# Layer 1's convolution stage: two gate tiles computed as one Strassen pair, with the conditioning tiles moved to an earlier stage

## The chip, the cores and the metric

The kernel runs on one core of a Trainium2 chip. The time is the device time of one execution in microseconds (us); the time before is the median of three runs. TensorE is PE in the rows (its weight loads are PEld), VectorE is DVE, ScalarE is ACT, GpSimd is POOL and the queue that issues the weight loads is SP.

## What is computed

The reference is two transformer blocks in fp32, with model width 1024 and 256 tokens: `first_block` (four mixer branches, a merge, a feed-forward part), then `second_block`, which runs two layers over 256 context tokens and 256 latent tokens. In the second of these layers (layer 1) only the 256 latent tokens are still needed. The part at issue is the mixer's convolution branch and the gated sums beside it:

```python
def _conv_module(glu, p):
    a, g = jnp.split(glu, 2, axis=-1)
    y = a * jax.nn.sigmoid(g)
    y = lax.conv_general_dilated(y, p['conv_w_dw'], (1,), [(pad, pad)], ...)   # depthwise, 31 taps
    y = jax.nn.silu(_layernorm(y, p['conv_ln_g'], p['conv_ln_b']))
    return y @ p['w_conv_o']
...
    g_att, g_gla, g_conv = jnp.split(jax.nn.sigmoid(gates), N_BRANCH_2, axis=-1)
    return (g_att * y_att + g_gla * y_gla + g_conv * y_conv) @ p['w_out']
```

Here `glu` and `gates` are columns of one projection of the normalised input, and `y_att`, `y_gla` are projections of the attention's and the recurrence's output. Apart from that, `silu(c) @ w_ada` gives the modulation of the layer norms; it needs only the condition vectors.

## The kernel before

Activations lie feature-major: a tile is 128 features on the partitions by the tokens, eight tiles are a full width of 1024. Weights come from a stream of tiles of 128 output features by 1024 inputs (512 KB) into eight slots `W[0]` to `W[7]`; SP issues the load of a slot when the counter `unit` says that the tile before it there has been used. `project` (L609 to L617, matmuls on L613) multiplies one weight tile by eight chunks of the input: 8 matmuls, each of which is two records in the trace.

The program is a list of phases, each with a number of turns, and every engine has a function for each phase. Each engine runs its own instructions in the order in which its function writes them, with waits on counting semaphores in between: `done` waits for this turn's event, `before` for that of the turn before, `earlier` for one of an earlier phase. Most phases begin with a wait for all engines (`phase_done`); PE goes ahead of it in those that are listed under `ahead`, the convolution stage among them.

The phases that matter here:
- `merge1` (first block): 16 tiles of gated sums in Strassen products over 128 columns (`product`, L841, and the loop on L891); a turn of it makes one tile.
- `gla`: the recurrence. Its last instruction on DVE is L3588.
- `conv`, layer 1: 8 turns, one for each tile of 128 channels. On PE (L1690) six tiles of weights by 256 tokens: the two halves of the GLU, gate and projection of the attention, gate and projection of the recurrence. ACT (L2348) makes three sigmoids (L2352, L2356). DVE (L3591) makes the GLU product (L3598), the 31 taps in two alternating sums (L3609, L3611, L3613), adds them up (L3616, L3618), handles one tile of `w_ada` (`ada_tile`, `ada_keep`, L2652 to L2671), and makes the gated sums into `MX` (L3626, L3629, L3630).
- `conv_norm`, layer 1: the mean over the convolution's output (L1784), the norm, and the eight tiles of the third gate on PE. Two of these stand ahead of the mean.
- `conv`, layer 0, computes its six tiles, over 512 tokens, with Strassen pairs already (`conv_strassen` on PE and ACT, sums of weights on L3637 to L3642).

A Strassen pair takes two weight tiles a and b (rows of a 2 x 2 block matrix, whose columns are the even and odd chunks of the inputs) and the left and right half of the tokens. Seven products of four matmuls each over half the tokens take the place of eight. They need four sums of weights (`w_summed0`), four sums of the input (`t_summed`), and copies of an accumulating bank at three points, which ACT makes (`hold`).

Of the kernel before, what the change touches and what calls it, by code (L numbers as in the profile page):

```python
# [19 lines left out]
ALU = mybir.AluOpType  # L20
# [3 lines left out]
P = 128  # L24
D = 1024
KC = D // P
# [25 lines left out]
ADA_TURNS = {"out1": (2, 0, 4), "down1": (4, 0, 5), "attend": (3, 0, 4), "attend_last": (3, 0, 4), "up2": (10, 0, 2),  # L52
             "attend1": (2, 0, 4), "attend1_last": (2, 0, 4), "conv1": (8, 0, 1)}
# [155 lines left out]
def program(nc, params, consts, stream, ada, cond, x_in, mem_in, ctx_in, out, counted):  # L209
    plan = phases()  # L210
    with ExitStack() as ctx:
# [302 lines left out]
        def split(c0):  # L514
# [23 lines left out]
        H_SUMS, G_SUMS = 17, 17 + 4 + 2 * QUADS  # L538
# [4 lines left out]
                 for v in (SQF, WORK[:, 2048:6144])]  # L543
        q_parts = [[v[:, i * S:(i + 1) * S].rearrange("p (j t) -> p j t", j=2) for i in range(8)]
                   for v in (WORK[:, 0:2048], MXF[:, 2048:4096])]
        conv_even, conv_odd = ([YG[:, FT * T2 + (2 * i + p) * S:FT * T2 + (2 * i + p + 1) * S] for p in range(2)]
# [58 lines left out]
        def _(pe):  # L605
# [1084 lines left out]
            def conv(s):  # L1690

                cols = slice(first_column(s.layer), T2)
                n = T2 - cols.start
                pe.wait_ge(*s.before("glu"))
                for u in range(2):
                    project(s, u, bank[u][:, 0:n], cols)
                pe.wait_ge(*s.earlier("gla_end", 0))
                for b in range(2):
                    pe.wait_ge(*s.before(f"gate{b}"))
                    project(s, 2 + 2 * b, bank[2 + 2 * b][:, 0:n], cols)  # L1700
                    pe.wait_ge(*s.before(f"mixed{b}"))
                    project(s, 3 + 2 * b, bank[3 + 2 * b][:, 0:n], cols, src=Y2[b])
# [68 lines left out]
            def conv_norm_first(s):  # L1771
# [3 lines left out]
                def gate(c):  # L1775
                    project(s, c, bank[2 + (c + 3 + s.layer) % 6][:, 0:n], cols)

                one, two = (2, 3) if s.layer else (4, 5)
                for c in range(one):
                    if s.layer == 0:  # L1780
                        pe.wait_ge(*s.earlier(("acc_taken0", "first_taken0", "cross_taken0", "acc_taken1")[c], 0))
                    gate(c)
# [5 lines left out]
                for c in range(two, KC):  # L1788
                    if c >= 6:
# [7 lines left out]
                     "gla": (gla_begin, gla_middle, gla_end), "conv": conv, "merge2": merge2, ("merge2", 0): merge_strassen,  # L1797
# [10 lines left out]
        def _(act):  # L1808
# [393 lines left out]
            def layernorm(s, dest, scale, shift):  # L2202
# [17 lines left out]
                for c in range(KC if conv else LATE):  # L2220
# [5 lines left out]
                    if conv:  # L2226
# [3 lines left out]
                        act.activation(sg_conv[:, c, 0:n], bank[2 + (c + 3 + s.layer) % 6][:, 0:n], ACT.Sigmoid)\  # L2230
# [117 lines left out]
            def conv(s):  # L2348
# [82 lines left out]
        def _(dve):  # L2431
# [241 lines left out]
            def merge1(s):  # L2673
# [77 lines left out]
                for t in range(1, 16):  # L2751
# [12 lines left out]
                    if t == 3:  # L2764
                        condition()
# [1219 lines left out]
```

## Time and profile before

| | |
|---|---|
| median of 3 runs | 3032.07 us (3031.69 to 3032.41) |
| the profiled execution | 3033.64 us, its span 3031.8 us |
| PE busy | 2973.9 us, 98% of the span |
| DVE busy | 1909.4 us, 63% |
| ACT busy | 739.2 us, 24% |
| granted TensorE clock | 0.998 of full speed |
| PE's share of the chain that ended last | 94% |

The span is the part of the execution in which engines worked; 1.8 us of the execution's time lie around it. Busy time of PE is modelled, so a busy PE is not PE at its peak, and successive rows of PE overlap: the pace is read from the distance between starts. "x16" is a number of records merged into one row.

### The profile page before, as it was taken

How to read it: one execution, taken by the hardware profiler on the slowest of the kernel's cores; microseconds unless marked ns; L12 is line 12 of the kernel's file. 1: busy time of each engine (PE TensorE's matmuls, PEld its weight loads, DVE VectorE, ACT ScalarE, POOL GpSimd, SP SyncE). 2: the span in 40 equal slices, each digit the busy share in tenths (PEclk: the TensorE clock that was granted, in tenths of full speed). 3: DMA queues.
4: the chain of work that ended last, by engine and by line, in shares of the span. 5: the costliest groups of instructions: out<-in, count | busy, mean ns of one | idle time of the engine just before them, and what ended most of it. 6: DMA issues, size and time to landing. Idle time of an engine off the chain costs nothing.

```text
span 3031.8 us, 45316 instructions
## 1 busy us (share of the span) xinstructions
PE 2973.9 (98%) x15958; PEld 2451.2 (81%) x15958; DVE 1909.4 (63%) x3765; ACT 739.2 (24%) x1786; POOL 62.8 (2%) x109
## 2 busy tenths in 40 slices
PE   9999999999999999999999999999999999999998
PEld 8888889989985566667775888888866778887998
DVE  4456326667656777768886566665357667863665
ACT  3334212212213333311113041110043431021111
POOL 0000000000010000000000000000000000000000
PEclk9999999999999999999999999999999999999999
DMA  5243334554562311112222114332223123434443
GB/s 194 93 149 111 139 125 168 170 208 163 198 227 104 127 53 50 63 63 83 83 83 89 63 49 146 125 125 90 90 92 119 65 86 129 176 132 153 153 150 115
DMA packets 105049, 363.97 MB, mean 120 GB/s; under 512 B 11488, under 2 KB 17632, under 8 KB 104800
## 3 DMA queue, kind: packets, MB, share of 16 engines
q1 hardware_dynamic: 90832, 310.94, 29.5%
q0 software_dynamic: 14096, 51.39, 4.8%
q8 instruction: 80, 1.31, 0.2%
q14 instruction: 41, 0.34, 0.0%
HBM read 361.23 MB, written 1.05 MB: 119 GB/s over the span
## 4 chain that ended last, share of the span: by engine, by line
PE 94%; DVE 3%; issue 1%; ACT 1%; DMA 1%; DVEq 0%; ACTq 0%; SPq 0%
PE bank L613 25%; PE bank L1126 7%; PE bank L1290 6%; PE bank L1708 5%; PE bank L841 5%; PE bank L1365 4%; PE bank L1592 4%; PE bank L1483 3%; PE bank L624 3%; PE bank L1606 2%; PE bank L1302 2%; PE bank L1456 2%; PE bank L1045 1%; PE bank L1651 1%; PE bank L1168 1%
## 5 line engine op out<-in xcount | busy, mean ns | idle before, releaser
L613 PE MATMUL bank<-H,W 128*128 128x256 f32 (+1 forms) x2048 | 497.3, 400 | 2.9 <-issue 2.8
L613 PEld LDWEIGHTS bank<-H,W 128*128 128x128 f32 x2048 | 386.9, 190 | 99.8 <-issue 52.0
L613 PE MATMUL bank<-YG,W 128*128 128x256 f32 (+1 forms) x912 | 258.9, 439 | 1.3 <-issue 0.8
L613 PEld LDWEIGHTS bank<-YG,W 128*128 128x128 f32 x912 | 172.9, 190 | 74.0 <-issue 56.6
L1483 PE MATMUL bank<-H,W 128*128 128x512 f32 (+1 forms) x320 | 119.4, 509 | 2.5 <-ACT H L2224 2.5
L1592 PE MATMUL bank<-W,H 128*128 128x256 f32 x512 | 118.8, 383 | 0.0
L1592 PEld LDWEIGHTS bank<-W,H 128*128 128x128 f32 x512 | 96.0, 193 | 13.8 <-issue 1.9
L1290 PE MATMUL bank<-MX,SQ 128*128 128x256 f32 x480 | 105.2, 379 | 0.0
L1290 PEld LDWEIGHTS bank<-MX,SQ 128*128 128x128 f32 x480 | 91.2, 190 | 12.4
L1483 PEld LDWEIGHTS bank<-H,W 128*128 128x128 f32 x320 | 58.8, 190 | 45.1 <-issue 38.2
L3655 DVE SCALAR_TENSOR_TENSOR YG<-WORK,PR,YG 128x512 f32 (+1 forms) x120 | 89.7, 747 | 0.0
L624 PEld LDWEIGHTS bank<-W,H 128*128 128x128 f32 x768 | 88.7, 192 | 0.8
L624 PE MATMUL bank<-W,H 128*128 128x128 f32 x768 | 89.0, 275 | 0.0
L1606 PE MATMUL bank<-H,W 128*128 128x512 f32 (+1 forms) x256 | 87.9, 486 | 0.0
L3655 DVE SCALAR_TENSOR_TENSOR WORK<-WORK,PR 128x512 f32<-128x512 f32 x112 | 83.7, 747 | 0.0
L1811 ACT ACT_TABLE_LOAD x21 | 26.9, 1283 | 213.7 <-DVEq L309 211.6
L1126 PE MATMUL bank<-H,W 128*128 128x128 f32 x640 | 77.7, 275 | 0.0
L1126 PEld LDWEIGHTS bank<-H,W 128*128 128x128 f32 x640 | 74.7, 192 | 0.1
L324 ACT ACTIVATE WORK<-bank,rowmax 128x128 f32<-128x128 f32 (+2 forms) x88 | 46.1, 530 | 117.3 <-DVE rowmax L317 117.3
L1708 PE MATMUL bank<-H,W 128*128 128x256 f32 x320 | 71.8, 379 | 0.3 <-issue 0.3
L1302 PE MATMUL bank<-H,W 128*128 128x256 f32 x320 | 70.8, 379 | 0.5 <-issue 0.5
L317 DVE TENSOR_REDUCE rowmax<-bank 128x1 f32<-128x128 f32 (+2 forms) x88 | 41.2, 494 | 46.0 <-PE bank L785 24.8
(633 smaller groups left out, 5841.8 us busy)
## 6 DMA issues: line engine op xcount, KB each, us to landing
W<-stream SPq DMA_DIRECT2D x556, 512.0 KB, 3.3
WORK<-ada POOLq DMA_DIRECT2D x44, 512.0 KB, 4.5
YG<-ada POOLq DMA_DIRECT2D x40, 512.0 KB, 3.6
W<-stream SPq DMA_DIRECT2D x24, 384.0 KB, 3.7
SQ<-ada POOLq DMA_DIRECT2D x12, 512.0 KB, 7.2
W<-stream SPq DMA_DIRECT2D x16, 128.0 KB, 2.3
CN<-consts SPq DMA_DIRECT2D x1, 1984.0 KB, 15.5
X<-x_in SPq DMA_DIRECT2D x2, 512.0 KB, 5.4
```

The costliest lines, as they stand in the source:

```text
L613: m = pe.matmul(out_ap, W[u][:, c, :], src[:, c, cols], start=first and c == 0, stop=last and c == k - 1)
L624: m = pe.matmul(o, H[:, c, col0 + t * P:col0 + (t + 1) * P], W[u][:, c, :], start=c == 0, stop=c == KC - 1)
L841: m = pe.matmul(out, w[:, c, :], b[:, c, :], start=first and c == 0, stop=c == KC // 2 - 1, skip_group_check=True)
L1126: m = pe.matmul(out, w[:, c, :], b[:, c, :], start=first and c == 0, stop=c == KC // 2 - 1, skip_group_check=True)
L1290: m = pe.matmul(out, w[:, c, :], b[:, c, :], start=first and c == 0, stop=c == KC // 2 - 1, skip_group_check=not first)
L1302: m = pe.matmul((acc, top)[c % 2][j], W[j][:, c, :], H[:, c, left], start=c < 2, stop=c >= KC - 2)
L1365: ends[q] = pe.matmul(out, w[q][:, c, :], b[:, 4 * q + c, :], start=first and q == 0 and c == 0, stop=q == 2 and c == n - 1, skip_group_ch ...
L1483: m = pe.matmul(out_bank[:, 0:T2 - cols.start], W[i][:, c, :], H[:, c, cols], start=c == 0, stop=c == KC - 1)
L1592: m = pe.matmul(o, H[:, c, t * P:(t + 1) * P], slots[:, 3:5, c, :], start=c == 0, stop=c == KC - 1)
L1606: m = pe.matmul(bank[6 + u][:, 0:n], W[5 + u][:, c, :], H[:, c, c0:T2], start=c == 0, stop=c == KC - 1)
L1708: m = pe.matmul(out, w[:, c, :], b[:, c, :], start=first and c == 0, stop=c == KC // 2 - 1, skip_group_check=not first)
L3655: o = dve.scalar_tensor_tensor(sums[tap % 2], src, w, sums[tap % 2], ALU.mult, ALU.add)
```

## The change

- `conv`, layer 1: the two gate tiles (slots 0 and 4) become one Strassen pair over two halves of 128 tokens. The other four tiles stay as they were. The GLU tiles (slots 2 and 3) stand at the beginning of a turn's loop body; the pair and the attention's projection for the next turn are opened at its end. The stream's order of tiles is changed to match.
- ACT: three copies and four sigmoids of 128 columns and one sigmoid of 256 per turn, instead of three sigmoids of 256.
- DVE: four sums of weights per turn, three sums that take the products out of the banks, and the taps in pieces between them: 3, 3, 6, 8 and 11. The pieces of 8 and 11 stand behind the first sum of the next turn's pair.
- The eight tiles of `w_ada` that this stage handled go to `merge1`, one in each of eight turns, with their loads (issued by POOL).
- `conv_norm`, layer 1: three tiles of the third gate ahead of the mean instead of two.

Cut to its core:

```diff
-ADA_TURNS = {"out1": (2, 0, 4), "down1": (4, 0, 5), "attend": (3, 0, 4), "attend_last": (3, 0, 4), "up2": (10, 0, 2),
-             "attend1": (2, 0, 4), "attend1_last": (2, 0, 4), "conv1": (8, 0, 1)}
+MERGE_ADA = (4, 5, 7, 8, 9, 11, 12, 13)
+ADA_TURNS = {"merge1": (8, 0, 1), "out1": (2, 0, 4), "down1": (4, 0, 5), "attend": (3, 0, 4), "attend_last": (3, 0, 4), "up2": (10, 0, 2),
+             "attend1": (2, 0, 4), "attend1_last": (2, 0, 4)}
...
+            def conv_halves():
...
+                def open_pair(s, begins=False):
+                    acc, top, cross = (bank[5 + i][:, 0:P] for i in range(3))
...
+                    product(acc, a[:, EVEN, :], H[:, EVEN, left], first=True).then_inc(*s.tick("p10"))
...
+                    pe.wait_ge(*s.before("first_taken0"))
+                    product(top, a[:, ODD, :], H[:, ODD, left], first=True).then_inc(*s.tick("p20"))
+                    pe.wait_ge(tally.sem("t_summed"), CONV_SUMS + 2)
+                    pe.wait_ge(*s.done("p1_held0"))
+                    pe.wait_ge(*s.done("w_summed0", 1))
+                    product(acc, sums[1], late_t[1]).then_inc(*s.tick("v20"))
+                    pe.wait_ge(*s.before("cross_taken0"))
+                    pe.wait_ge(*s.done("w_summed0", 3))
+                    product(cross, sums[0], late_t[0], first=True).then_inc(*s.tick("unit"))
+                    pe.wait_ge(tally.sem("t_summed"), CONV_SUMS + 3)
+                    pe.wait_ge(*s.done("v2_held0"))
+                    for c in range(KC // 2):
+                        m = pe.matmul(acc, sums[2][:, c, :], late_t[2][:, c, :], start=False, stop=c == KC // 2 - 1,
...
+                    m.then_inc(*s.tick("v30"))
...
+                def close_pair(s):
...
+                    product(acc, W[4][:, ODD, :], late_t[3]).then_inc(*s.tick("unit"))
+                    pe.wait_ge(*s.done("corner_taken0"))
+                    product(cross, conv_w[0][3], H[:, ODD, right]).then_inc(*s.tick("c120"))
...
+                def rest(s):
+                    pe.wait_ge(*s.before("glu"))
+                    project(s, 2, bank[2][:, 0:S], XS)
+                    project(s, 3, bank[3][:, 0:S], XS)
+                    close_pair(s)
+                    pe.wait_ge(*s.before("mixed1"))
+                    project(s, 5, bank[1][:, 0:S], XS, src=Y2[1])
+
+                def middle(s, following):
+                    rest(s)
+                    open_pair(following)
+                    pe.wait_ge(*following.before("mixed0"))
+                    project(following, 1, bank[0][:, 0:S], XS, src=Y2[0])
+
+                return lambda s: open_pair(s, begins=True), middle, rest
...
+                one, two = (3, 4) if s.layer else (4, 5)
                 for c in range(one):
...
+            def conv_halves(s):
+
+                def hold(made, to):
+                    act.activation(to, bank[5][:, 0:P], ACT.Copy).then_inc(*s.tick(f"{made}_held0"))
+
+                def sigmoid(ap, name, src=None, scale=1.0):
+                    act.activation(ap, ap if src is None else src, ACT.Sigmoid, scale=scale).then_inc(*s.tick(name))
+
+                act.wait_ge(*s.done("p10"))
+                act.wait_ge(*s.before("corner_taken0"))
+                hold("p1", late_gate_held[:, 0, :])
+                act.wait_ge(*s.done("first_taken0"))
+                sigmoid(late_gate[:, near], "gate_sig0")
+                act.wait_ge(*s.done("v20"))
+                act.wait_ge(*s.before("cross_taken0"))
+                hold("v2", late_gate_held[:, 1, :])
+                act.wait_ge(*s.done("v30"))
+                hold("v3", late_gate_held[:, 0, :])
+                act.wait_ge(*s.done("corner_taken0"))
+                sigmoid(late_two[:, far], "gate0", scale=-1.0)
-                    act.wait_ge(*s.done("unit", 2 + 2 * b))
-                    act.wait_ge(*s.before(f"mixed{b}"))
-                    act.activation(sg2[:, b, 0:n], bank[2 + 2 * b][:, 0:n], ACT.Sigmoid).then_inc(*s.tick(f"gate{b}"))
+                sigmoid(conv_sg[:, 0:S], "glu_sig", src=bank[2][:, 0:S])
+                act.wait_ge(*s.done("unit", 4))
+                act.wait_ge(*s.before("mixed1"))
+                sigmoid(late_two[:, near], "acc_taken0", src=bank[5][:, 0:P], scale=-1.0)
+                act.wait_ge(*s.done("cross_taken0"))
+                sigmoid(late_gate[:, far], "gate_sig0")
 
             def conv_strassen(s):
...
+                    if t in MERGE_ADA:
+                        ada_tile("merge1", MERGE_ADA.index(t), 0)
+                        ada_keep("merge1", MERGE_ADA.index(t))
...
+            def late_sums(f):
+                a, b, sums, made = W[0], W[4], conv_w[0], "w_summed0"
+                dve.wait_ge(*f.done("loaded0"))
+                dve.wait_ge(*f.done("loaded4"))
+                dve.wait_ge(*f.before("c120"))
+                dve.tensor_tensor(sums[0], b[:, EVEN, :], b[:, ODD, :], ALU.add).then_inc(*f.tick(made))
+                dve.wait_ge(*f.done(made, 0))
+                dve.tensor_tensor(sums[1], sums[0], a[:, EVEN, :], ALU.add).then_inc(*f.tick(made))
+                dve.tensor_tensor(sums[2], a[:, EVEN, :], b[:, EVEN, :], ALU.add).then_inc(*f.tick(made))
+                dve.wait_ge(*f.done(made, 1))
+                dve.tensor_tensor(sums[3], sums[1], a[:, ODD, :], ALU.add).then_inc(*f.tick(made))
...
+            def late_first(f):
+                dve.wait_ge(*f.done("p20"))
+                dve.wait_ge(*f.done("p1_held0"))
+                dve.tensor_tensor(late_gate[:, near], late_gate_held[:, 0, :],
+                                  bank[6][:, 0:P], ALU.add).then_inc(*f.tick("first_taken0"))
...
+            def late_begin(f):
+                for at in (0, PAD + S):
+                    dve.memset(padded[:, 1, at:at + PAD], 0.0).then_inc(tally.sem("padding"), 1)
+                late_sums(f)
+                sum_blocks(late_t, tally.sem("t_summed"), CONV_SUMS, sides=(left, right))
+                dve.wait_ge(tally.sem("padding"), 4)
+                late_first(f)
+                late_corner(f)
+
+            def late_middle(s, f):
+                late_glu(s)
+                late_taps(s, 0, 3)
+                late_gate_cross(s)
+                late_taps(s, 3, 6)
+                late_mix_att(s)
+                late_sums(f)
+                late_mix_gla(s)
+                late_taps(s, 6, 12)
+                late_first(f)
+                late_taps(s, 12, 20)
+                late_corner(f)
+                late_taps(s, 20, CONV)
+
+            def late_end(s):
+                late_glu(s)
+                late_taps(s, 0, 3)
+                late_gate_cross(s)
+                late_taps(s, 3, 6)
+                late_mix_att(s)
+                late_taps(s, 6, 14)
+                late_mix_gla(s)
+                late_taps(s, 14, CONV)
 
             def conv_sums(f, j):
                 a, b, sums, made = W[3 * j], W[3 * j + 2], conv_w[j], f"w_summed{j}"
...
+            pool.wait_ge(tally.sem("ada_done"), 1)
+            load_ada("merge1", 0, ("merge1", "out1"), cond_raw)
...
+            out += [tiles[n] for n in ((2, 3, 1, 0, 4, 5) if l else (2, 3, 4, 1, 5, 0))]
         out += [unit(w, gate + 2 * D + i * P) for i in range(8)]
```

ACT, the loop body of `conv`, layer 1. Names before the brackets are outputs and inputs, in the brackets stands what is waited for; `unit` counts finished weight tiles. Before:

```order
L2351 REGISTER_ALU [waits unit]
L2352 ACTIVATE WORK<-bank1 128x256 [waits glu]
L2354 REGISTER_ALU
L2355 REGISTER_ALU [waits unit]
L2356 ACTIVATE WORK<-bank2 128x256 [waits mixed0]
```

And in the changed kernel (`p10`, `v20`, `v30` are PE's first, third and fifth product of the pair, `first_taken0` is DVE's sum L3710):

```order
L2408 ACTIVATE WORK<-bank5 128x128 [waits corner_taken0,p10]
L2416 REGISTER_ALU
L2411 ACTIVATE WORK<-WORK 128x128 [waits first_taken0]
L2408 ACTIVATE WORK<-bank5 128x128 [waits cross_taken0,v20]
L2408 ACTIVATE WORK<-bank5 128x128 [waits v30]
L2411 ACTIVATE WORK<-WORK 128x128 [waits corner_taken0]
```

The copy that waits for `v20` stands behind a sigmoid that waits for `first_taken0`.

PE, layer-1 `conv`, from the attention's projection on. Before:

```order
L611 ISA [waits mixed0]
L613 MATMUL bank3<-YG,W 128x256 [waits loaded3]
L613 MATMUL bank3<-YG,W 128x256 x7
L1699 REGISTER_ALU
L611 ISA [waits gate1]
L613 MATMUL bank4<-H,W 128x256 [waits loaded4]
```

In the changed kernel, the opening of the next turn's pair from its second product on (`v2_held0` is ACT's second copy):

```order
L1698 MATMUL bank6<-H,W 128x128 [waits first_taken0]
L1698 MATMUL bank6<-H,W 128x128 x3
L1720 ISA [waits p1_held0,t_summed]
L1698 MATMUL bank5<-SQ,W 128x128 [waits w_summed0]
L1698 MATMUL bank5<-SQ,W 128x128 x3
L1723 REGISTER_ALU [waits cross_taken0]
L1698 MATMUL bank7<-SQ,W 128x128 [waits w_summed0]
L1698 MATMUL bank7<-SQ,W 128x128 x3
L1728 MATMUL bank5<-SQ,W 128x128 [waits v2_held0,t_summed]
L1728 MATMUL bank5<-SQ,W 128x128 x3
```

Whole tiles waited for loads and for events of the turn before; of the short products, three now wait for copies and sums made in the same turn.

DVE, the middle of the changed loop body, from the sums of weights to the first gated sums:

```order
L3675 TENSOR_TENSOR W<-W 128x512 [waits c120,loaded4]
L3676 ISA
L3677 TENSOR_TENSOR W<-W 128x512 [waits w_summed0]
L3678 TENSOR_TENSOR W<-W 128x512
L3679 REGISTER_ALU
L3680 TENSOR_TENSOR W<-W 128x512 [waits w_summed0]
L3730 REGISTER_ALU
L3731 REGISTER_ALU [waits unit]
L3732 REGISTER_ALU [waits acc_taken0]
L3733 TENSOR_TENSOR WORK<-WORK,bank1 128x256 [waits gate0]
```

Six taps follow (L3693), and then the sum that ACT's sigmoid waits for:

```order
L3693 ISA [waits dve]
L3693 SCALAR_TENSOR_TENSOR WORK<-WORK,PR 128x256
L3710 TENSOR_TENSOR WORK<-WORK,bank6 128x128 [waits p1_held0,p20]
L3687 REGISTER_ALU
L3693 ISA [waits dve]
```

The first of these sums waits for the load of slot 4, which PE frees in the same turn; before, DVE waited for no load here but that of the `w_ada` tile.

## Rows read from the trace of the kernel before

**Rows 1.** The page: busy time of the engines (us, share of the span, instructions).
```profile
PE 2973.9 (98%) x15958; PEld 2451.2 (81%) x15958; DVE 1909.4 (63%) x3765; ACT 739.2 (24%) x1786; POOL 62.8 (2%) x109
```
**Rows 2.** Busy time by stretch in the layer-1 stage (us and records, clock, DMA share, GB/s).
```profile
2580.00:2600.00 20.00, 20.00 (x95) 17.61 (x94) 16.69 (x44) 1.15 (x3) 0.53 (x1) 1.00 0.49 175
```
**Rows 3.** The chain that ended last, layer-1 `conv` into `conv_norm` (start, us, what).
```profile
2528.37 166.02 PE bank L613 x768
...
2694.50 7.17 PE bank L613 x32
2701.67 0.43 PE bank L1784 x2
```
**Rows 4.** Timeline, PE, two tiles of 256 columns in layer-1 `conv`.
```profile
2600.99 3.62 PE L613 MATMUL bank<-YG,W 128*128 128x256 f32 x16
2604.44 3.62 PE L613 MATMUL bank<-H,W 128*128 128x256 f32 x16
```
**Rows 5.** Timeline, `merge1`: products of 128 columns, and ACT's copy behind one.
```profile
560.36 1.06 PE L841 MATMUL bank<-YG,W 128*128 128x128 f32 x8
...
568.40 1.06 PE L841 MATMUL bank<-H,W 128*128 128x128 f32 x8
...
568.60 0.38 ACT L2000 ACTIVATE WORK<-bank 128x256 f32<-128x256 f32 x1 [3.19 <-PE bank L891]
```
**Rows 6.** Groups of PE: the dearest large group of 128-column matmuls.
```profile
L1651 PE MATMUL bank<-SQ 128*128 128x128 f32 x336 | 46.6, 275 | 1.9 <-DVE SQ L3554 1.9
```
**Rows 7.** Timeline, DVE, one turn of layer-1 `conv`.
```profile
2598.55 0.42 DVE L3598 TENSOR_TENSOR WORK<-WORK,bank 128x256 f32<-128x256 f32 x1
2599.28 0.41 DVE L3609 TENSOR_SCALAR YG<-WORK,PR 128x256 f32 x1 [0.31 <-DVE WORK L3598]
...
2599.87 0.48 DVE L3613 SCALAR_TENSOR_TENSOR YG<-WORK,PR,YG 128x256 f32 x1
2600.26 0.48 DVE L3613 SCALAR_TENSOR_TENSOR WORK<-WORK,PR 128x256 f32<-128x256 f32 x1
...
2612.59 1.23 DVE L2660 SCALAR_TENSOR_TENSOR WORK<-WORK,cond_row 128x1024 f32<-128x1024 f32 x1 [0.23 <-DVE tile_sum L3618]
...
2615.13 0.17 DVE L2669 COPY MOD<-ada_sums 128x2 f32 x1 [0.16 <-DVE WORK L2662]
...
2616.24 0.42 DVE L3629 TENSOR_TENSOR WORK<-WORK,bank 128x256 f32<-128x256 f32 x1 [0.19 <-DVE MX L3626]
2616.70 0.42 DVE L3630 TENSOR_TENSOR MX<-MX,WORK 128x256 f32 x1
```
**Rows 8.** Timeline, layer-0 `conv`: DVE's four sums of weights, to the next tap.
```profile
1355.99 0.69 DVE L3637 TENSOR_TENSOR WORK<-W 128x512 f32<-128x512 f32 x1
...
1358.53 0.74 DVE L3655 SCALAR_TENSOR_TENSOR WORK<-WORK,PR 128x512 f32<-128x512 f32 x1
```
**Rows 9.** Issues of weight loads with median us to landing: layer-1 `conv`, then `merge1`.
```profile
W<-stream SPq DMA_DIRECT2D x50, 512.0 KB, 3.2
...
W<-stream SPq DMA_DIRECT2D x32, 512.0 KB, 4.4
```
**Rows 10.** Timeline, layer-0 `conv`: a copy of a bank behind a waiting sigmoid on ACT.
```profile
1345.09 3.62 PE L1708 MATMUL bank<-H,W 128*128 128x256 f32 x16
...
1346.79 0.42 DVE L3671 TENSOR_TENSOR WORK<-WORK,bank 128x256 f32<-128x256 f32 x1
1347.24 0.42 ACT L2364 ACTIVATE WORK<-WORK 128x256 f32<-128x256 f32 x1 [11.89 <-DVE WORK L3671]
1347.62 0.38 ACT L2361 ACTIVATE WORK<-bank 128x256 f32<-128x256 f32 x1
```
**Rows 11.** Timeline, DVE in `merge1`: the idle time of a turn, a sum of 128 columns.
```profile
569.01 0.42 DVE L2705 TENSOR_TENSOR WORK<-WORK,bank 128x256 f32<-128x256 f32 x1 [3.42 <-ACT WORK L2000]
...
573.21 0.28 DVE L2729 TENSOR_TENSOR WORK<-WORK,bank 128x128 f32<-128x128 f32 x1
```
**Rows 12.** Timeline: DVE's last instruction ahead of layer-1 `conv`.
```profile
2529.87 0.69 DVE L3588 TENSOR_TENSOR YG<-WORK 128x512 f32 x1 [0.16 <-DVE WORK L3585]
```

More of the change, by code:

```diff
@@ L545, in program @@
                    for v in (WORK[:, 0:2048], MXF[:, 2048:4096])]
+        late_t = [SQF[:, i * 512:(i + 1) * 512].rearrange("p (c t) -> p c t", c=KC // 2) for i in range(4)]
+        late_gate, late_gate_held, late_two = work(3072, S), work(1856, 2, P), work(3584, S)
+        near, far = slice(0, P), slice(P, S)
         conv_even, conv_odd = ([YG[:, FT * T2 + (2 * i + p) * S:FT * T2 + (2 * i + p + 1) * S] for p in range(2)]
@@ L1775, in gate @@
                 def gate(c):
-                    project(s, c, bank[2 + (c + 3 + s.layer) % 6][:, 0:n], cols)
-                one, two = (2, 3) if s.layer else (4, 5)
+                    project(s, c, bank[2 + (c + 3 - s.layer) % 6][:, 0:n], cols)
+                one, two = (3, 4) if s.layer else (4, 5)
                 for c in range(one):
@@ L2655, in ada_tile @@
                 u = slot + k
[L2656 to L2657 removed]
+                tile = {"merge1": cond_raw}.get(name, att_ada_w if name.startswith("attend") else ada_w)[u]
+                junk = {"up2": ada_w[5], "merge1": cond_raw[1]}.get(name, att_ada_junk if name.startswith("attend") else ada_junk)
                 dve.wait_ge(tally.sem("ada_done"), turn * count + (first + k + 1))
@@ L3608, in conv @@
                     if tap == 0:
-                        o = dve.tensor_scalar(sums[0], src, w, par(f"conv_b{s.layer}", s.turn), ALU.mult, ALU.add)
+                        o = dve.tensor_scalar(sums[0], src, w, par("conv_b1", s.turn), ALU.mult, ALU.add)
                     elif tap == 1:
@@ L3614, in conv @@
                     o.then_inc(*s.tick("dve"))
[L3615 to L3630 removed]
+                if high == CONV:
+                    dve.wait_ge(*s.so_far("dve"))
+                    link(s, dve.tensor_tensor(sums[0], sums[0], sums[1], ALU.add))
+                    link(s, dve.tensor_tensor(tile_sum[:, XS], tile_sum[:, XS], sums[0], ALU.add))
@@ L3861, in weight_stream @@
                 tiles += [unit(w, gate + n * D + i * P), unit(a[name][l], i * P)]
-            out += tiles if l else [tiles[n] for n in (2, 3, 4, 1, 5, 0)]
+            out += [tiles[n] for n in ((2, 3, 1, 0, 4, 5) if l else (2, 3, 4, 1, 5, 0))]
         out += [unit(w, gate + 2 * D + i * P) for i in range(8)]
```

121 lines of the change are left out of this document (64 added, 57 removed).

## The prediction

> **What bounds the kernel now.** I read the page first: TensorE is busy for 98% of the span [rows 1]. Then the busy time by stretch, for the stage that is changed: 20.00 us of 20.00 on TensorE, 16.69 on VectorE, 1.15 on ScalarE, at full clock [rows 2]. Last the chain and the timeline. The chain through the stage is TensorE alone, 768 records in 166.02 us [rows 3], and two tiles of 256 columns start 3.45 us apart [rows 4]; 48 of these make 165.6 us, so there is nothing between them. Nothing that VectorE or ScalarE does here is waited for. A change pays in this stage by what it takes off TensorE, as long as TensorE goes on waiting for nobody. What one kernel can be told from another by is about 0.2%, 6 us.
>
> **TensorE's work.** In `merge1`, nine blocks of four matmuls over 128 columns lie between the starts of the first two of [rows 5], 8.04 us: 0.893 us a block, 0.1116 a record. Two whole tiles (6.90 us) become seven such blocks (6.25 us): 0.65 us less per turn, 5.2 us in eight. That is all that the change can give, 0.17%. If 128-column records cost what they do in the dearest large group, 46.6 us by 336, or 0.139 us [rows 6], the pair would cost 7.8 us and the stage 7.0 us more than before; that group has waits in it, while the products in `merge1` are the same code, so I take 0.893.
>
> The Trainium skill, "TensorE: Matmul & The Clock Gate", section "Back-to-back issue gap", says that in a stream of weight loads and matmuls 128 columns cost about 81 ns where the column count alone gives about 56. By that rule the 448 records (8 turns, 7 blocks, 8 records) would cost 11 us more than their columns do (an estimate from the page's figures), and the stage would be about 4 us slower than before for it. This trace does not agree: half of the 256-column record is 0.108 us, and the 128-column record is 0.112.
>
> **The path through one opened pair.** The clock starts with a turn's first GLU tile on TensorE. The second GLU tile ends at 6.90, the two closing products at 8.69, the recurrence's projection at 12.14, and the first four products of the next pair at 15.71. There the fifth product wants to start. It waits for ScalarE's second copy (`v2_held0`). In ScalarE's order this copy stands behind a sigmoid that waits for `first_taken0`, and VectorE makes that sum only after half a turn's work. So VectorE's way from the GLU product to this sum is followed step by step:
> - The product starts 0.20 us after TensorE's tile ends (the delay from a TensorE block to ScalarE in [rows 5]), at 7.10; the first tap 0.73 later, at 7.83 [rows 7].
> - Three taps, 0.59 for the first two and 0.39 for one at the steady pace [rows 7]: 8.82. The cross sum waits for the second closing product, 8.69 and 0.20, and takes 0.28 [rows 11]: 9.2.
> - Three taps, 1.19, and the first gated sum, 0.42 like L3630: 10.8.
> - The sums of weights need slot 4, whose old tile TensorE uses until 7.79. The load is issued at about 8.0. Landing takes 3.2 us where loads are 3.45 us apart, and 4.4 where they come in bunches [rows 9]; here slot 3's load is 0.9 us ahead. I take 3.9: 11.9. VectorE stands still for 1.1 us.
> - Four sums of weights, 2.54 [rows 8]: 14.4. Two instructions for the second gated sum, 0.19, 0.46 and 0.42 [rows 7]: 15.5. Six taps, 2.38: 17.9. The sum for `first_taken0`, 0.28 [rows 11]: 18.2.
> - On ScalarE the sigmoid and the copy behind it, 0.76 us over 256 columns [rows 10]; these have half the columns, so I take 0.6, and 0.1 to TensorE: 18.85.
>
> TensorE therefore stands still from 15.71 to 18.85, **3.1 us per turn**, in the seven turns that open a pair. If the load were there when VectorE comes to it, the stall would be 2.0; with a landing of 4.4 us it is 3.7. VectorE's own work (31 taps 12.1 us, the other sums some 6.5) fits into the turn, so it is not the amount that binds but the place of this one sum.
>
> **The ends of the stage.** Before, TensorE starts the stage at 2528.37 [rows 3], while VectorE finishes the recurrence at 2530.56 [rows 12]. The changed TensorE has 0.89 + 3.45 + 0.89 us to do, to 2533.6. VectorE needs until about 2531.2 for the phase's start and two memsets, 2.54 for the sums of weights and 1.4 for the first two sums of inputs, which have the same size: 2535.2. TensorE waits 1.7 us, and some 0.2 at the fifth product. I take 1.9, between 1 and 3. At the end VectorE needs to about 22.9 us on the last turn's clock; TensorE ends the projection at 12.14 and three gates (10.35) at 22.5: 0.4 us of waiting, with two gates it would be 3.9. That is what the third gate is for. After the mean there is one gate less to cover the norm: between nothing and 3.45 us. Four gates, 13.8 us, remain over it; I take nothing and keep 3 us for the range.
>
> **The `w_ada` tiles.** They take VectorE 2.7 us from the first product's start to the copy's end, 2.9 with the waits [rows 7]. In the stage they leave, VectorE isn't waited for, so their going brings nothing by itself; it makes the room for the sums. In `merge1` VectorE is idle for 3.42 us in a turn before the sum that follows [rows 11]: they fit, with 0.5 us left. I cost this at nothing; were the cover 0.5 us short in each of the eight turns, it would be 4 us at most. POOL's eight loads move from one stage to the other; one of them has most of a turn (14 blocks, 12.5 us) to land, and 0.5 MB there beside 2 MB of weights is what the bunches of [rows 9] already bear: nothing, too.
>
> **Sum.** -5.2 (products), +21.9 (seven stalls of 3.13), +1.9 (start), +0.4 (end): **+19.0 us**. The profiled execution took 3033.64 us, its span 3031.8; the changed one would take 3052.6. The median of the runs is 1.6 us under the profiled one, so the number for the runs is 3051. With stalls of 2.0 and 3.7 us the sum is +11 and +23, or 3043 and 3055; with 2 us less and 3 us more for the ends and the norm, 3041 and 3058.
>
> **The rivals.**
> - *The wait costs nothing, and the time is not slower.* The copy waits for `first_taken0` only by its place in ScalarE's order, since their data have nothing in common. If VectorE ends that sum before 15.1 on the turn's clock (15.71 less 0.6 for ScalarE), the fifth product is on time. That needs 3.1 us off VectorE's way, and then -5.2 + 1.9 + 0.4 = -2.9 gives 3029. For it: the way is summed up from single instructions and could be too long. Against it: six taps and four sums of weights alone are 4.9 us, and they come after the cross sum, which can't start before 8.9: 13.8 at the earliest, without anything else between; and a copy behind a waiting sigmoid is seen in [rows 10]. There the first product of a block of 16 ended at about 1346.8 (eight records of 0.216), yet the copy of it started at 1347.62, 0.4 us after the sigmoid ahead of it, which had waited for VectorE. Chance 0.11.
> - *The load is the later one.* Slot 4 is freed at 7.79, and if its load lands 5 us or more after its issue, it holds the sums of weights, and with them the third product too: from 12.6 on TensorE waits there as well. Each 0.1 us more costs 0.7 us in all. At 5.4 us the stall is 4.6, the turn 24.7 and the time 3061. For it: two loads at once; against it: the bunches of `merge1` land in 4.4. Chance 0.03.
> - *Short products are dear.* At the 0.139 us of [rows 6] the time would be 3051 + 12.2 = 3063. Against it: [rows 5]. Chance 0.01.
> - *The change doesn't take effect:* the order of the engines shows all of it, so this has no chance.
>
> **How the numbers follow.** The stall has a chance of 0.85, and its time, 3051, is the prediction. The range is its own, 3041 to 3058; left out are the rival at 3029 and the dearer ones above, 0.15 in all, and what I may have misjudged at its edges. Slower by over 0.2% (above 3038): 0.85 + 0.03 + 0.01 - 0.01 for a stall under 1.3 us = 0.88. Within 0.2%: the rival at 3029 and this rest, less what falls below 3026: 0.11. Faster by over 0.2% needs 6.1 us where TensorE gives up 5.2: 0.01.
>
> **What the changed profile would show.** In the chain, a turn of about 23.2 us, where it was 20.7. TensorE idle for about 3 us before the fifth product of each pair (L1728), with ScalarE as what it waited for, and ScalarE's sigmoid and copy (L2411, L2408) back to back just before. VectorE idle for about 1.1 us before L3675 on the load of slot 4, and about 3 us before the GLU product. 128-column blocks 0.89 us apart. `merge1` as long as before. I am wrong if turns of 20.1 us appear, if TensorE waits at the third product instead, or if `merge1` grows.

## The result, and the profile after

| | before | changed | forecast |
|---|---|---|---|
| median of the runs, us | 3032.24 (3031.60 to 3033.27, 6 runs) | 3059.08 (3057.52 to 3063.79, 6 runs) | 3051, range 3041 to 3058 |
| ratio | | 1.0091, 95% interval 1.0078 to 1.0104 | |
| the profiled execution | 3033.64, span 3031.8 | 3058.51, span 3056.7 | 3052.6 |

The change costs 26.8 us. Four executions of over 3300 us, two of the kernel before and two of one version below, are left out of all medians here. The forecast had the direction and the mechanism, and 7.8 us too little; the time lies 1 us above the upper end of the range.

The page of the changed kernel, busy time of the engines, against [rows 1]:

```profile
PE 2976.7 (97%) x16150; PEld 2456.2 (80%) x16150; DVE 1933.8 (63%) x3811; ACT 748.8 (24%) x1826; POOL 64.6 (2%) x109
```

TensorE is busy for 2.8 us more, although it has 5.2 us less to do: the first sign that some of its work ran slower. The rest of the 25 us of span is idle time. It all lies in one stage. From the last matmuls of the recurrence to the first of `merge2` it was 198.3 us (2526.80 to 2725.12), and is now 225.1 (2524.58 to 2749.63), 26.7 more. Ahead of the stage the changed kernel's profiled execution is 2.2 us shorter, most of it because the clock fell there once in the execution before; behind the stage it is 0.4 longer.

The chain of waits through one turn of the changed stage (start, us, what), where [rows 3] was TensorE alone:

```profile
2590.74 0.91 PE bank L1698 x8
2591.81 4.38 DMA W<-stream
...
2598.83 0.34 DVE WORK L3733
2599.71 0.23 issue
2601.92 0.29 DVE WORK L3710
2602.25 0.19 issue
2602.45 0.27 ACT WORK L2408
2602.85 2.04 PE bank L1728 x8
2604.89 12.30 PE bank L617 x48
```

A turn is now a circle. TensorE's first closing product frees slot 4; its load lands after 4.4 us; VectorE makes the sums of weights, the gated sums, six taps and the sum on L3710; ScalarE makes the sigmoid and the copy (L2408); and TensorE goes on at the fifth product (L1728). In the seven turns the load takes 4.4 to 5.0 us of this chain. It was 0 of it before.

The waits of the stage (engine line waited for: us in total, times, longest):

```profile
PE bank L1728 <- ACT WORK L2408: 19.6, 7, 2.8
DVE W L3675 <- DMA W<-stream: 14.3, 7, 2.4
```

The timeline of the same turn, VectorE and ScalarE (start, us busy, what, [idle before]):

```profile
2596.21 0.69 DVE L3675 TENSOR_TENSOR W<-W 128x512 f32<-128x512 f32 x1 [1.83 <-DMA W<-stream]
...
2601.92 0.28 DVE L3710 TENSOR_TENSOR WORK<-WORK,bank 128x128 f32<-128x128 f32 x1
...
2602.23 0.31 ACT L2411 ACTIVATE WORK<-WORK 128x128 f32<-128x128 f32 x1 [5.04 <-DVE WORK L3710]
2602.45 0.26 ACT L2408 ACTIVATE WORK<-bank 128x128 f32<-128x128 f32 x1
```

The copy is the case of [rows 10] again: its product had ended at about 2598.8 (the third product starts at 2597.68), and it waits for 3.6 us behind a sigmoid that waits for VectorE. The Trainium skill, "PSUM — Partial Sum Buffer", section "Engine vs sequencer instructions", says "ScalarE/VectorE/GpSimdE queues are strict FIFO"; the trace agrees, with those 3.6 us.

The wait before L1728 is only the last part of a turn's stall: the third product had already started 0.1 to 0.7 us late for the sums of weights, by the distance of the starts.

TensorE in two turns, one with the clock up and one with it down:

```profile
2574.09 2.36 PE L1698 MATMUL bank<-SQ,W 128*128 128x128 f32 x16 [0.19 <-DVE W L3677]
2579.25 1.13 PE L1728 MATMUL bank<-SQ,W 128*128 128x128 f32 x8 [2.80 <-ACT WORK L2408]
2580.22 3.62 PE L617 MATMUL bank<-YG,W 128*128 128x256 f32 x16
...
2602.85 2.04 PE L1728 MATMUL bank<-SQ,W 128*128 128x128 f32 x8 [2.80 <-ACT WORK L2408]
2604.68 5.60 PE L617 MATMUL bank<-YG,W 128*128 128x256 f32 x16
```

The idle time is 2.80 us in both. After the second, eight records take 2.04 us in place of 1.13 and sixteen 5.60 in place of 3.62. The granted clock by stretch (the last three columns: clock, DMA share, GB/s) shows the same:

```profile
2580.00:2600.00 20.00, 19.95 (x116) 17.86 (x114) 14.18 (x36) 1.84 (x6) 0.00 (x0) 1.00 0.39 131
2600.00:2620.00 20.00, 17.20 (x79) 15.24 (x79) 13.28 (x36) 2.03 (x7) 0.00 (x0) 0.83 0.30 105
2620.00:2640.00 20.00, 17.07 (x90) 15.10 (x89) 15.38 (x38) 1.73 (x6) 0.00 (x0) 0.91 0.29 105
2640.00:2660.00 20.00, 17.08 (x104) 15.33 (x103) 15.13 (x38) 1.93 (x7) 0.00 (x0) 1.00 0.38 131
```

A stretch at 0.83 is one that is partly at full speed (2.4 GHz) and partly at half (1.2 GHz). The turns, from closing product to closing product, are 24.20, 23.86, 26.45, 25.27, 23.76, 23.82 and 23.66 us, 171.0 in all. TensorE's work in them is 7 x 20.05 = 140.4. Of the 30.7 us between, the five turns at full clock give 3.81 for a stall, 26.7 in seven, and 4.0 are the clock in two turns (2.6 and 1.4). The runs suggest that this cost varies: the six lie 6 us apart, and the two slowest, 3061.9 and 3063.8 us, have a mean granted clock of 0.996 and 0.995 where the others have 0.997. Those of the kernel before lie within 1.7 here, and within 2.8 in the larger sets used below.

Such a fall stood in the trace of the kernel before as well, in another stage. There TensorE waits 3.69 us in front of L1365, and 44 records take 11.44 us. In the version with the other parts alone (below) the same records follow a wait of 3.19 us and take 9.76:

```profile
2066.28 11.44 PE L1365 MATMUL bank<-YG,W 128*128 128x256 f32 x44 [3.69 <-DVEq L309]
```
```profile
2065.59 9.76 PE L1366 MATMUL bank<-YG,W 128*128 128x256 f32 x44 [3.19 <-DVEq L310]
```

The granted clock of the kernel before is 0.91 from 2060 to 2080. Of the thirteen profiles read here, eight have this fall and five do not.

### The profile page after: what moved, and what is told of

It is laid out like the page before. It is cut to its first block, busy times and chain, and to the rows that moved or that the text cites. A ratio compares the mean times of both kernels' runs of the same rounds, so it can differ in the third digit from the quotient of the medians.

```text
span 3056.7 us, 45806 instructions
## 1 busy us (share of the span) xinstructions
PE 2976.7 (97%) x16150; PEld 2456.2 (80%) x16150; DVE 1933.8 (63%) x3811; ACT 748.8 (24%) x1826; POOL 64.6 (2%) x109
## 4 chain that ended last, share of the span: by engine, by line
PE 91%; DVE 4%; DMA 2%; issue 2%; ACT 1%; DVEq 0%; SPq 0%; ACTq 0%
PE bank L617 22%; PE bank L1130 7%; PE bank L1294 6%; PE bank L1763 5%; PE bank L845 5%; PE bank L1369 4%; PE bank L1596 4%; PE bank L1487 3%; PE bank L628 3%; PE bank L1610 2%; PE bank L1306 2%; DMA W<-stream 2%; PE bank L1460 2%; PE bank L1049 1%; PE bank L1655 1%
## 5 line engine op out<-in xcount | busy, mean ns | idle before, releaser
L617 PE MATMUL bank<-H,W 128*128 128x256 f32 (+1 forms) x1792 | 440.6, 403 | 2.5 <-issue 2.4
L617 PEld LDWEIGHTS bank<-H,W 128*128 128x128 f32 x1792 | 338.1, 190 | 92.6 <-issue 51.2
L1487 PEld LDWEIGHTS bank<-H,W 128*128 128x128 f32 x320 | 58.8, 190 | 45.2 <-issue 38.2
L1130 PEld LDWEIGHTS bank<-H,W 128*128 128x128 f32 x640 | 74.7, 192 | 0.1
```

Of the source, the lines that this page charges most:

```text
L617: m = pe.matmul(out_ap, W[u][:, c, :], src[:, c, cols], start=first and c == 0, stop=last and c == k - 1)
L1130: m = pe.matmul(out, w[:, c, :], b[:, c, :], start=first and c == 0, stop=c == KC // 2 - 1, skip_group_check=True)
L1487: m = pe.matmul(out_bank[:, 0:T2 - cols.start], W[i][:, c, :], H[:, c, cols], start=c == 0, stop=c == KC - 1)
```

## The experiments

The theory on which they rest: the stall comes from the place of ScalarE's second copy behind the sigmoid, and VectorE's way to the sum that this sigmoid needs; and TensorE's idle time brings its clock down, for another 4 us. The rivals: the load of slot 4 by itself, VectorE's amount of work, and falls of the clock that have nothing to do with the change. The versions ran on three chips, each beside the kernel before. Its median is 3033.4 us beside the copy ahead of the sigmoid, the taps in the wait, the idle products in the stall, and the projection first with ScalarE's order mended. It is 3033.6 beside the sum first, the projection first with ScalarE's order as in the change, two gates, and the other parts. It is 3033.2 beside the other three: the repeat, the idle products ahead of the mean, and the start order. Ratios are to it; the changed kernel's own 26.8 us are to 3032.2.

**The copy ahead of the sigmoid.** On ScalarE alone:

```diff
                 act.wait_ge(*s.done("p10"))
                 act.wait_ge(*s.before("corner_taken0"))
                 hold("p1", late_gate_held[:, 0, :])
-                act.wait_ge(*s.done("first_taken0"))
-                sigmoid(late_gate[:, near], "gate_sig0")
                 act.wait_ge(*s.done("v20"))
                 act.wait_ge(*s.before("cross_taken0"))
                 hold("v2", late_gate_held[:, 1, :])
+                act.wait_ge(*s.done("first_taken0"))
+                sigmoid(late_gate[:, near], "gate_sig0")
```

> ScalarE's second copy (v20) stands ahead of the sigmoid that waits for first_taken0; nothing else is changed. Theory (the copy's place in ScalarE's order is the wait): TensorE no longer idles before the fifth product (L1728). What is left in a turn is about 0.5 us at the third and fourth product, for the sums of weights behind the load of slot 4 (landed 12.7 us on the turn's clock, two sums 14.0, four sums 15.3, where TensorE is there at 13.9 and 15.1). Turn 20.6 us in place of 23.7 and more, no fall of the granted clock: 3059 - 7 x 3.3 - 4 = 3032 us. Rival, the load of slot 4 is what binds: the idle time goes to the third and fourth product at nearly its old size, time above 3050. Rival, VectorE's amount of work binds: the turn stays over 22 us, time above 3045.

Measured: 3034.6 us, 24.5 less than the changed kernel. The timeline of TensorE in it:

```profile
2612.83 2.36 PE L1698 MATMUL bank<-SQ,W 128*128 128x128 f32 x16 [0.35 <-DVE W L3677]
2615.03 1.06 PE L1728 MATMUL bank<-SQ,W 128*128 128x128 f32 x8
```

The idle time before L1728 is gone in all seven turns, and so are the falls of the clock. A turn is 20.7 to 21.3 us: TensorE now waits for the sums of weights behind the load, where 0.5 us a turn were expected and 0.8 are there on average (20.88 less 20.05). So the load binds only next. VectorE's amount of work doesn't bind: it is the same as in the changed kernel.

**Taps in the time in which VectorE waits for the load.**

```diff
-                late_sums(f)
-                late_mix_gla(s)
-                late_taps(s, 6, 12)
+                late_taps(s, 6, 10)
+                late_sums(f)
+                late_mix_gla(s)
+                late_taps(s, 10, 12)
```

> Four taps (6 to 9) move ahead of the sums of weights, into the time in which VectorE waits for slot 4; nothing else is changed. Theory (VectorE's way to the sum first_taken0 sets the stall, and the wait for the load is a part of that way): four taps are 1.57 us and VectorE waits 2.0 there, so the sum comes 1.6 us earlier; the stall before L1728 falls by 1.6 us in each of seven turns, 11 us, and 0 to 4 us more if the granted clock falls less often: 3044 to 3048. Rival, VectorE's amount of work binds: no change, 3059. Rival, the load binds TensorE itself: no change, 3059.

Measured: 3044.2 us, 14.9 less. TensorE waits 1.22 us before L1728 in each of the seven turns, where it was 2.80:

```profile
2598.06 1.13 PE L1728 MATMUL bank<-SQ,W 128*128 128x128 f32 x8 [1.22 <-ACT WORK L2408]
```

That is 1.58 us, four taps of 0.395; 11.1 in seven turns. The other 3.8 fit the clock, which doesn't fall in this stage of its profile. VectorE's wait for the load lay on the path.

**The sum first, the taps behind it.**

```diff
                 late_mix_gla(s)
-                late_taps(s, 6, 12)
                 late_first(f)
-                late_taps(s, 12, 20)
+                late_taps(s, 6, 20)
```

> VectorE makes the sum first_taken0 right behind the second gated sum, ahead of the six taps (6 to 11) instead of behind them; the order on ScalarE and TensorE is that of the changed kernel. Theory (the stall is VectorE's way to this sum, because of the copy's place behind the sigmoid): the sum comes 2.4 us earlier and so does the copy; of the 2.8 us of idle time before L1728 some 0.4 are left, and the granted clock doesn't fall: 3059 - 7 x 2.4 - 4 = 3038 us. Rival (VectorE's amount of work, which is the same here): 3059 us.

Measured: 3038.5 us, with 0.43 us before L1728 in all seven turns. Nothing but the place of one sum of 0.28 us among VectorE's instructions is worth 20 us here.

**Idle products in the stall.** On TensorE, ahead of the wait for `v2_held0` and not in the stage's first opening:

```diff
+                    if not begins:
+                        for _ in range(12):
+                            pe.matmul(bank[4][:, 0:P], ident, ident, start=True, stop=True)
                     pe.wait_ge(tally.sem("t_summed"), CONV_SUMS + 3)
                     pe.wait_ge(*s.done("v2_held0"))
```

> Twelve 128x128 products of the identity into an unused bank stand on TensorE before its wait for v2_held0, in the seven turns that open a pair: 24 records of 0.112 us, 2.7 us of work in about 3 us of idle time. The wait itself is as long. Theory (the granted clock fell because TensorE stood idle for 2.8 us in a turn, and that cost 4 us beside the stalls): granted clock 1.00 in all of the stage, turns of 23.7 to 23.9 us all seven, time 3055 us and runs closer together than the 6 us of the changed kernel. Rival (the falls have nothing to do with the idle time): 3059 us, with turns of 25 to 26 us as before.

Measured: 3055.5 us, the four runs within 2.2, all at a mean clock of 0.998 or 0.999. In the timeline the idle products fill the stall (L1727), the fifth product still starts 5.2 us after the third, as above, and the tile behind it takes 3.62 us; the stretch at 0.83 before is at 1.00:

```profile
2598.00 2.36 PE L1698 MATMUL bank<-SQ,W 128*128 128x128 f32 x16
2600.20 2.84 PE L1727 MATMUL bank<-CN 128*128 128x128 f32 x24
2603.17 1.13 PE L1731 MATMUL bank<-SQ,W 128*128 128x128 f32 x8
2604.13 3.62 PE L617 MATMUL bank<-YG,W 128*128 128x256 f32 x16
```
```profile
2600.00:2620.00 20.00, 19.88 (x119) 18.06 (x118) 14.38 (x38) 2.03 (x7) 0.00 (x0) 1.00 0.39 131
```

The seven turns add up to 167.4 us in place of 171.0. So some 3.6 to 4 of the 26.8 us are the clock, and the idle time is what brought it down. (Against the kernel before on each chip, the loss goes from 26.8 to 22.1 us; the two medians of that kernel differ by 1.1.) The Trainium skill, "TensorE: Matmul & The Clock Gate", section "HAM oscillation — how this bites in real kernels", tells of a matmul kernel in which a wait for a DMA in every tile brings the clock down every time. Here a wait for ScalarE did so in two stalls of seven in the profiled execution.

**The projection before the pair is opened, with ScalarE's order mended too.** The attention's projection becomes slot 0 and the gate's tile slot 1:

```diff
-                    open_pair(following)
                     pe.wait_ge(*following.before("mixed0"))
-                    project(following, 1, bank[0][:, 0:S], XS, src=Y2[0])
+                    project(following, 0, bank[0][:, 0:S], XS, src=Y2[0])
+                    open_pair(following)
```

> Two edits: ScalarE's second copy ahead of the waiting sigmoid, and on TensorE the attention's projection (now slot 0) before the pair is opened (now slot 1), so that the pair's third product is wanted 3.45 us later. Theory: the sums of weights (ready 14.0 and 15.3 us on the turn's clock) are early for products at 17.4 and 18.3, the copy isn't waited for, and nothing stalls: turns of 20.05 us, 5.2 us less in the stage and 1.2 us lost at its start: 3028 to 3029 us, within 0.2% of the kernel before and under it. Rival (VectorE can't keep up with a turn of 20.05 us): VectorE's idle time before the GLU product goes to nothing and the turn stays above 20.7, time above 3033.

Measured: 3029.4 us, ratio 0.9986 (0.9977 to 0.9995). Nothing stalls, and a turn is 20.07 us:

```profile
2602.65 1.05 PE L1698 MATMUL bank<-SQ,W 128*128 128x128 f32 x8
...
2613.13 1.95 PE L1698 MATMUL bank<-SQ,W 128*128 128x128 f32 x16
2614.91 1.06 PE L1728 MATMUL bank<-SQ,W 128*128 128x128 f32 x8
2615.81 7.07 PE L617 MATMUL bank<-H,W 128*128 128x256 f32 x32
2622.72 1.05 PE L1698 MATMUL bank<-SQ,W 128*128 128x128 f32 x8
```

This is the -5.2 of the products less 1.2 for the start. VectorE keeps up, though barely: from the second turn on its GLU product starts 0.3 to 0.65 us behind its own last sum, and not because TensorE's tile is late. What is left to it is its wait for slot 4, 0.4 to 2.5 us a turn. In the profile of the repeat below that wait is 3.25 us in one turn, and in the next turn TensorE waits 0.52 us for VectorE's gated sum before the attention's projection.

**The projection first, ScalarE's order as in the change:**

> The attention's projection before the pair is opened, as in b1, but with ScalarE's order of the changed kernel (the copy behind the waiting sigmoid). Theory: the fifth product is wanted at 19.2 us on the turn's clock in place of 15.7, and the copy is there at 19.2 to 19.4: a stall of 0.1 to 0.2 us a turn, 3030 to 3031 us. If the copy's place counted by itself, and not only against the time at which the product is wanted, the time would stay above 3040.

Measured: 3031.2 us. TensorE still waits before L1728 in three turns, 0.38, 0.20 and 0.17 us:

```profile
2616.14 1.13 PE L1728 MATMUL bank<-SQ,W 128*128 128x128 f32 x8 [0.20 <-ACT WORK L2408]
```

The copy stands in the same bad place as before, and costs 0.4 us at most, because its product is wanted 3.45 us later. Either cure alone takes off the loss; with the copy moved alone 1.2 us are left.

**Two gates ahead of the mean.** The projection first and ScalarE's order mended, and `one, two = (2, 3)` in `conv_norm`:

> b1 with two tiles of the third gate ahead of the mean instead of three. In b1 TensorE ends the third at 2698.9, and VectorE's last sum ends at 2698.4: with two, TensorE would stand still for 3.45 - 0.5 = 2.95 us before the mean, and the gate that is moved behind it hides 0.5 us of the gap before merge2 at most: 3029.4 + 2.5 to 3.0 = 3032 us. If the third gate only changed the order of work that is hidden anyway: 3029.4.

Measured: 3034.5 us, 5.1 more than with three (4.9 when each is taken against the kernel before on its chip), where 2.5 to 3.0 were expected. TensorE around the mean (L1841), here and then with three gates:

```profile
2700.10 1.22 PE L1841 MATMUL bank<-tile_sum,CN 128*128 128x256 f32 x2 [2.99 <-DVEq L310]
2701.11 4.71 PE L617 MATMUL bank<-H,W 128*128 128x256 f32 x16
```
```profile
2698.89 0.59 PE L1841 MATMUL bank<-tile_sum,CN 128*128 128x256 f32 x2
2699.32 3.62 PE L617 MATMUL bank<-H,W 128*128 128x256 f32 x16
```

The stall is 2.99 us, as expected; behind it the clock falls again: the two rows take 0.6 and 1.1 us longer.

**The same with idle products in that stall**, beside the best version so far on the same chip:

```diff
+                if s.layer:
+                    pe.wait_ge(*s.earlier("mixed0", 0))
+                    for _ in range(12):
+                        pe.matmul(bank[0][:, 0:P], ident, ident, start=True, stop=True)
                 pe.wait_ge(tally.sem("phase_done"), WORKERS * s.number)
```

> b1 once more on another chip, as the base of the two runs beside it: 4 us under the kernel before, ratio 0.9986 or 0.9987.

Measured: 3029.2 us, ratio 0.9985 (0.9976 to 0.9994).

> b3 with twelve 128x128 products of the identity on TensorE in the 2.99 us in which it stood idle before the mean. In b3 the mean and the tile behind it took 1.22 and 4.71 us where b1 has 0.59 and 3.62, about 1.7 us at the lower clock. Theory (the idle time brought the clock down): the stall stays 2.9 us, the tile behind the mean takes 3.62 us, and the time is b1 + 3.0 = 3032.5, where b3 had b1 + 5.1. Rival (chance falls of the clock): b1 + 5.

Measured: 3031.6 us, 2.4 over the version beside it where 3.0 were expected and 5.1 without the products. The mean (L1845 here) and the tile behind it:

```profile
2695.26 2.84 PE L1843 MATMUL bank<-CN 128*128 128x128 f32 x24
2698.44 0.70 PE L1845 MATMUL bank<-tile_sum,CN 128*128 128x256 f32 x2 [0.34 <-DVEq L310]
2698.98 3.62 PE L617 MATMUL bank<-H,W 128*128 128x256 f32 x16
```

The same wait, without the slow tile. This is the second place in which idle products take away what a stall costs beyond its own length. The two versions differ by 2.9 us, though (2.5 against the kernel before on each chip), and the slow rows above account for 1.7; runs of one version lie 2 to 4 us apart, so I don't read more into it.

**The other parts without the pair:** the kernel before, with the `w_ada` tiles in `merge1` and three gates ahead of the mean.

> The kernel before with the other parts of the change and no pair: the eight w_ada tiles in merge1, three tiles of the third gate ahead of the mean. Theory: nothing waited for them before and the idle time of merge1 takes them, so no difference, within 1 us of the kernel before. Rival (the first block pays for the tiles): 2 to 4 us slower. Rival (VectorE's relief in the last turn brings the mean forward): up to 0.5 us faster.

Measured: 3031.8 us, ratio 0.9996 (0.9987 to 1.0005): the median is 1.8 us lower, and no difference is inside the interval. The loss is the pair's.

**VectorE's order at the start of the stage**, on top of the projection first and ScalarE's order mended (`early_blocks` makes the first two sums of inputs):

```diff
+                late_sums(f, between=early_blocks)
+                dve.tensor_tensor(t[2], b22, b12, ALU.subtract).then_inc(made, 1)
+                dve.wait_ge(made, CONV_SUMS + 2)
+                dve.scalar_tensor_tensor(t[3], t[1], -1.0, b21, ALU.mult, ALU.subtract).then_inc(made, 1)
                 for at in (0, PAD + S):
                     dve.memset(padded[:, 1, at:at + PAD], 0.0).then_inc(tally.sem("padding"), 1)
-                late_sums(f)
-                sum_blocks(late_t, tally.sem("t_summed"), CONV_SUMS, sides=(left, right))
```

> b1 with another order of VectorE's work at the start of the stage: the first two sums of weights, the first two sums of inputs, then the other sums of weights and of inputs, the memsets last. In b1 the third product waits 1.20 us for the second sum of inputs (ready 2532.6), which stands behind all four sums of weights. Theory (the start costs what VectorE's order makes it cost): the second sum of inputs is ready 1.3 us earlier, the third product waits for nothing, the fourth waits about 0.3 us for the last sum of weights: 0.9 us less than b1. Rival (the data of the stage before hold the sums): the wait stays 1.2 us.

Measured: 3028.1 us, ratio 0.9984 (0.9975 to 0.9993), the fastest version. The third to fifth product at the start (x16 is the third and fourth), first in the version it is made from, then in it:

```profile
2532.72 2.05 PE L1698 MATMUL bank<-SQ,W 128*128 128x128 f32 x16 [1.20 <-DVE SQ L3227]
2534.61 1.06 PE L1728 MATMUL bank<-SQ,W 128*128 128x128 f32 x8
```
```profile
2531.47 2.43 PE L1698 MATMUL bank<-SQ,W 128*128 128x128 f32 x16
2533.73 1.06 PE L1728 MATMUL bank<-SQ,W 128*128 128x128 f32 x8
```

The third product starts 1.25 us earlier, and the fifth 0.88, the 0.9 expected. The median is 1.1 us under that of the version beside it on the same chip, which two versions' runs don't tell from 0.9.

## Why the prediction was partly wrong

| term | forecast | measured | from |
|---|---|---|---|
| products | -5.2 | -5.2 | 20.07 us a turn without stalls, 128-column blocks 0.89 apart |
| seven stalls | +21.9 | +26.7 | 3.81 us each in turns at full clock |
| clock | none | +4.0 | two turns; +3.6 by the run with idle products |
| start | +1.9 | +1.2 | the wait for L3227 |
| end | +0.4 | 0.0 | the mean starts 0.1 us behind the last gate, as before |
| `w_ada` tiles, norm | 0 | 0 | the run of the other parts; 0.54 us before `merge2`, 0.57 before |
| sum | +19.0 | +26.7 | the medians differ by 26.8 |

- **Right: the mechanism.** The idle time stands before the fifth product, ScalarE's sigmoid and copy stand back to back ahead of it, and moving the one behind the other takes it away. That -5.2 us is all that the pair can give was right as well.
- **Wrong: the clock, a term put at nothing.** "At full clock" was read from [rows 2] as a property of the stage. It was one of a TensorE that doesn't wait. The sum put in seven waits of 3.1 us and kept the clock. This step alone is half of the miss: 4.0 of 7.8 us. A row for it was there to be read: the 3.69 us in front of L1365, with the slow records behind.
- **Mis-sized: the load of slot 4.** It was to be issued at 8.0 on the turn's clock and to land 3.9 us later, at 11.9, between the 3.2 and 4.4 of [rows 9]. It lands 4.4 to 5.0 us after its issue, and VectorE starts on the sums at 12.5 to 13.1, 12.75 on average (2596.21 less 2583.68 is the earliest). That is 0.85 us a turn, 6.0 in all; VectorE's way from there, 0.3 us shorter than forecast, gives 2.2 of it back, and the slower pace behind a stall (0.97 us from the fifth product to the next tile, where 0.89 is usual) is part of another 0.9. Together these are nearly all of the 4.8 us by which the stalls' term is larger. The rival on the load, at 5 us and more, had this step nearly right. Both medians were of other patterns of loads, and this one comes 0.9 us behind another; that this is the reason was not tried. That VectorE's way counts once per turn is shown by the run with taps in this wait.
- **Right step by step elsewhere.** From VectorE's start on the sums to the end of L3710 the forecast was 6.3 us (11.9 to 18.2), and it is 5.99 (2596.21 to 2602.20); from there to TensorE 0.65 forecast, 0.65 measured. The third product waited for the sums too, 0.1 to 0.7 us, inside the same chain.
- **The rival on VectorE's amount** was set aside rightly, but by less than the sum made it look: at 20.07 us a turn VectorE has nothing left but its wait for slot 4.
- **The rival on short products** set a busy time by record (0.139) against a pace (0.112). By the same measure the products in `merge1` (L841) have 47.5 us by 360, or 0.132, and still start 0.112 us apart; so the two figures were not of the same kind. The rival was set aside rightly all the same: blocks start 0.89 us apart in the changed stage.
- **The third gate** was costed as a cover of 3.5 us at the end; with two gates the version with the projection first took 5.1 us more, at least 1.7 of it the clock.
- **The range** was built from the bounds of the stall, the ends and the norm, all at full clock. With 4 us more for the clock it would have reached 3062 and held 3059.

## What to carry to other kernels

A short product that waits for a copy in its own turn is only as early as whatever stands ahead of that copy in its engine's order: go through that order for every wait on another engine, and either put the copy first or something long between the product that fills the bank and the one that wants the copy. When a change makes TensorE wait for some 3 us where it had not waited, add a term for the clock. And when a load becomes part of a circle through all engines, its landing time counts once per turn, so bound it by more than the median of another pattern.

## What the runs showed of the hardware

- Stalls of 2.8 us of TensorE were followed by records at about half rate in two cases of seven in one execution, and one of 2.99 us in the one profile of the version with two gates; stalls of 1.2 us and less in this stage never were, in the profiles taken. In front of L1365 (L1369 in the changed kernel), a stall of 3.2 to 3.7 us was followed by slow records in eight profiles of thirteen, at 1.7 to 3.0 us each. The execution before has a stretch at 0.97 (2345 to 2400), in the recurrence: there a tile behind an idle time of 1.90 us takes 5.31 us in place of 3.62, and the other profiles don't show a fall there. With 24 records of the identity in the stall the clock stayed at 1.00 in both places, in one profile each.
- The fall is not in every turn with the same stall, and the runs scatter: 6 us over six runs of the changed kernel, the slowest at the lowest mean clock, against 2 over four with the idle products.
- Two loads of 512 KB issued 0.9 us apart: the second landed 4.4 to 5.0 us after its issue. The median of all 50 loads is 3.3 us in this stage, and was 3.2 in the stage before, with loads 3.45 us apart.
